# One hybrid decoder step on one core: convolution taps dealt differently, the conv norm's channel sums one block later, the key turns placed among the chunk sums, and the GLA gate multiplied in ahead of its norm

## The chip, the cores and the metric

The kernel runs on one core of a Trainium2 chip. The metric is device microseconds of one launch. Everything is in f32; the products of activations with weights split each operand into a high part (type fp32r) and a rest and use three products.

## The reference, cut to what matters

There are 1024 prompt tokens and 8 sample tokens (T = 1032 columns). One layer is computed:

```python
proj = rms_norm(x) @ w_in          # c_val, c_gate, q, k, v, r, a_lr
u = c_val * sigmoid(c_gate)
conv = silu(layer_norm(depthwise_conv31(u) + b_dw))
log_a = log_sigmoid(a_lr @ w_alpha + b_alpha) / 16
o, S = gla(q / 8, k, v, log_a)     # S_t = diag(a_t) S_(t-1) + k_t v_t^T, o_t = q_t S_t
o = rms_norm(o, gla_g) * silu(r)   # per head of 128
x = x + concat(conv, o) @ w_out
x = x + cross_attn(rms_norm(x), memory keys, memory values)
x = x + relu(rms_norm(x) @ w_up)**2 @ w_down
y = rms_norm(x)
```

The gate silu(r), the gain gla_g and the factor of the norm are multiplied element by element, so that their order changes rounding alone.

## The kernel before, in words

Activations stand with features on the 128 partitions and the 1032 tokens along the free axis, in three blocks of 344 columns. A weight tile is [128, 8, 128]: 8 steps k over the input features, for 128 output features. A tile product is 8 x 3 x 3 = 72 matmuls into three banks of PS[0] or PS[1]. Each engine's program is written out by hand, in order, with semaphores between them.

For each weight tile t, SyncE (SP) loads it, ScalarE (ACT) makes the high part (`w_high`, L620) and GpSimd (POOL) the rest in two halves (`lo`, L557) into one of two slots, t % 2. `w_high(t)` waits until the product of tile t-2 is done, since it takes over that slot. In the stage of the output projection (tiles T_OUT to T_OUT+7) `w_high(t+2)` is the last thing that `residual_tile(t)` does on ACT, behind VectorE's (DVE) addition of tile t to the residual (L1745), ACT's operand copy and ACT's square.

**Input projection.** 21 tiles (I_A at 8, I_K 9, I_Q 11, I_V 13, I_R 17), each three blocks of 24 matmuls (`in_block`, L1162). `SLOTS` names what TensorE (PE) does between the blocks. From tile I_V on, each tile's blocks 1 and 2 are followed by a "unit": eight matmuls of 128 x 128 (`unit_scores`, L1132, 16 records) that give the GLA scores of one level of a binary tree for one pair of heads, in two banks M[0] and M[1], one per half g. A unit's half needs the bank that the half of the unit before left: DVE frees it for units 0 to 11 with a masked copy (`level_select`, L1633), ACT for units 12 to 15 (`block_select`, L798). DVE's `unit_step` is an update of q (L1609 to L1612), a select, an update of k (L1620) and the second select.

**Convolution.** 124 taps on DVE (4 channel tiles of 31, `TAPS`), each one instruction over 128 x 1024 (L1559 to L1563). `taps(n)` does the next n. Their counts decide what DVE does before which unit: 24 in the last round of `u_product`, 4 before `decay_tree`, 16 ahead of unit 0, and then 1, 5, 1, 5, 1, 5, 1, 5, 1, 7 behind units 0 to 9. Behind unit 10 come the sums over the four channel tiles (L1675 to L1677), which PE sums over the partitions (`channel_sum`, L1121, "mean" in SLOTS at tile I_R+2, block 0); behind unit 11 DVE centres (L1681), ACT squares (L850), DVE adds (L1689), PE sums again ("var", tile I_R+3, block 0), ACT makes the factor (L853, L854), DVE multiplies it in (L1693, behind unit 14) and ACT does the silu (L858).

**Between the projections.** PE turns the keys (`key_turn`, L1148, four of four transposes), ACT reads them to k_in (L682), PE makes each chunk's k v product (`chunk_sum`, L1231, 8 chunks), DVE the recurrent states (`state_after`, L1704 and L1708), PE the outputs (`outputs`, L1249 and L1251, four rounds of two chunks). DVE and ACT read each round to sc_t (L1717, L874) and ACT squares it into sq_t (L880). ACT copies the conv result as operand (`conv_high`, L862), POOL makes its rest (L573) and then the sample tokens' state: two products (L581), two (L586) and two sums (L589).

**GLA norm and output projection.** PE does, in this order: k 0 to 3 of tile T_OUT (the conv half); the sample outputs (`sample_out`, L1283); 12 products with ones that give the sums of squares of the 4 heads (L1294, one per block of 344, alternating between M[0] and M[1]); k 0 to 3 of tile T_OUT+1; k 4 to 7 of T_OUT, then k 4 to 7 of T_OUT+1; the six further tiles. ACT takes 12 logarithms (L892) and 4 exponentials (L897). Then, per head, DVE multiplies o by the factor (L1731, L1732), by gain and gate (L1735), ACT copies the high part (L902) and DVE makes the rest (L1490), which PE's k = 4 + h waits for. SP loads the residual x once the last gate is done.

## Time and profile before

| | us |
|---|---|
| three runs | 1565.95, 1568.66, 1574.23 (median 1568.66) |
| profiled execution, its own time | 1565.79 |
| its span | 1564.0 |
| PE busy | 1475.6 (94%) |
| PE weight loads busy | 1430.9 (91%) |
| DVE, ACT, POOL busy | 610.2 (39%), 451.9 (29%), 383.2 (25%) |
| mean granted clock of PE | 0.979 of full speed |

PE is busy from end to end but for the first tenth and for a stretch between some 250 and 470 us. A matmul shows its latency there, so that "busy" is not the array at its peak: PE's pace is read from how far apart its groups start. In the views below, times run from the start of the span.

### The profile page before, as it was taken

What the parts mean: (1) busy time and instruction counts of PE and PEld (TensorE: products, weight loads), DVE (VectorE), ACT (ScalarE), POOL (GpSimd) and SP (SyncE); (2) the same over time, 40 slices, a digit from 0 to 9 for tenths busy, and PEclk for the clock granted to TensorE, in tenths of its full rate; (3) what the DMA queues carried; (4) which work ended last, traced back from release to release, by engine and by line L of the source; (5) the groups of instructions that cost most, each with busy time, mean ns of one, the idle gap of its engine ahead of it and who ended that gap; (6) DMA issues with size and microseconds to landing.
All of it is one profiled execution on the core that took longest, in us unless ns stands there. A gap on an engine that the chain in (4) does not pass through costs nothing.

```text
span 1564.0 us, 22310 instructions
## 1 busy us (share of the span) xinstructions
PE 1475.6 (94%) x9454; PEld 1430.9 (91%) x9454; DVE 610.2 (39%) x649; ACT 451.9 (29%) x598; POOL 383.2 (25%) x292
## 2 busy tenths in 40 slices
PE   5899998998989999788999999999999999999994
PEld 5799997997769999677999999999999999999994
DVE  3759989895243345462231211122011211022123
ACT  5532252438252233341233211123011311022121
POOL 5753231213302222100222222222222222222220
PEclk9999999999989999999999999999999999999997
DMA  8411150012033341336111111111111111111102
GB/s 293 141 61 48 58 51 28 28 41 68 31 122 122 109 155 55 121 128 230 55 41 42 52 54 40 41 54 40 54 41 51 42 54 40 54 40 40 54 27 108
DMA packets 45273, 113.99 MB, mean 73 GB/s; under 512 B 7688, under 2 KB 20248, under 8 KB 43808
## 3 DMA queue, kind: packets, MB, share of 16 engines
q1 hardware_dynamic: 43312, 104.19, 21.0%
q10 hardware_dynamic: 1904, 8.98, 1.4%
q8 instruction: 44, 0.72, 0.2%
q14 instruction: 13, 0.11, 0.0%
HBM read 100.85 MB, written 12.30 MB: 72 GB/s over the span
## 4 chain that ended last, share of the span: by engine, by line
PE 80%; DVE 7%; issue 5%; ACT 3%; POOL 3%; DMA 1%; ACTq 0%; SPq 0%; DVEq 0%; POOLq 0%
PE ps L1061 63%; PE ps L1162 10%; DVE ps L1561 2%; POOL w_split L557 2%; PE m L1132 1%; PE m L1325 1%; PE ps L1359 1%; PE ps L1175 1%; ACT w_split L620 1%; DMA cache_b<-in_cache_v 1%; DVE x_res L1934 1%; POOL a_op L573 0%; DMA v_raw<-out_mv 0%; PE ps L1381 0%; DVE x_in L1527 0%
## 5 line engine op out<-in xcount | busy, mean ns | idle before, releaser
L557 POOL TENSOR_TENSOR w_split<-w_raw,w_split 128x512 fp32r<-128x512 f32 x234 | 324.8, 1409 | 1122.3 <-ACT w_split L620 1122.2
L1061 PE MATMUL ps<-a_op,w_split 128*128 128x344 f32 x3456 | 548.8, 321 | 8.1 <-DVE a_op L1490 6.3
L1061 PEld LDWEIGHTS ps<-a_op,w_split 128*128 128x128 f32 x3456 | 545.9, 189 | 9.9 <-issue 5.5
L1061 PE MATMUL ps<-b_op,w_split 128*128 128x344 f32 x2880 | 454.6, 319 | 0.0
L1061 PEld LDWEIGHTS ps<-b_op,w_split 128*128 128x128 f32 x2880 | 452.3, 188 | 0.8 <-issue 0.4
L1162 PE MATMUL ps<-a_op,w_split 128*128 128x344 f32 x1440 | 233.8, 322 | 0.0
L1162 PEld LDWEIGHTS ps<-a_op,w_split 128*128 128x128 f32 x1440 | 227.1, 188 | 1.9 <-issue 1.4
L620 ACT ACTIVATE w_split<-w_raw 128x1024 fp32r<-128x1024 f32 x117 | 122.8, 1050 | 239.3 <-PE ps L1061 239.1
L1561 DVE SCALAR_TENSOR_TENSOR ps<-conv_in,par,ps 128x1024 f32<-128x1024 f32 x116 | 149.6, 1290 | 3.7
L1905 DVE SCALAR_TENSOR_TENSOR tmp<-ps,rstd 128x1032 f32<-128x1032 f32 x32 | 39.5, 1233 | 215.1 <-PE ps L1061 203.2
L1915 DVE TENSOR_TENSOR x_res<-x_res,ps 128x1032 f32 x24 | 29.5, 1230 | 230.8 <-PE ps L1061 230.8
L1015 ACT ACTIVATE tmp<-tmp 128x1032 f32<-128x1032 f32 x32 | 34.1, 1067 | 259.1 <-DVE tmp L1905 259.1
L1745 DVE TENSOR_TENSOR x_res<-x_res,ps 128x1032 f32<-128x1032 f32 x24 | 29.5, 1229 | 163.6 <-PE ps L1061 163.6
L1061 PE MATMUL ps<-m_op,w_split 128*128 128x256 f32 x384 | 55.5, 304 | 21.9 <-POOL w_split L557 21.9
L1061 PEld LDWEIGHTS ps<-m_op,w_split 128*128 128x128 f32 x384 | 51.7, 208 | 25.1 <-issue 18.1
L1910 DVE TENSOR_TENSOR a_op<-tmp,a_op 128x1032 f32 x32 | 39.5, 1234 | 80.7 <-ACT a_op L1018 80.7
L909 ACT ACTIVATE b_op<-x_res,par 128x1032 fp32r<-128x1032 f32 x16 | 18.6, 1160 | 128.4 <-DVE x_res L1745 128.4
L666 ACT ACTIVATE tmp<-x_res 128x1032 f32<-128x1032 f32 x21 | 22.2, 1057 | 66.0 <-DVE x_res L1745 66.0
L1018 ACT ACTIVATE a_op<-tmp 128x1032 f32 x32 | 34.2, 1067 | 4.3
L1325 PE MATMUL m<-k_op,a_op 128*128 128x256 f32 x192 | 26.2, 292 | 6.7 <-ACT ex L944 6.7
L1325 PEld LDWEIGHTS m<-k_op,a_op 128*128 128x128 f32 x192 | 25.0, 197 | 7.8 <-ACT ex L944 7.2
L557 POOL TENSOR_TENSOR w_split<-w_more,w_split 128x512 fp32r<-128x512 f32 x16 | 25.0, 1586 | 16.3 <-ACT w_split L620 16.3
(200 smaller groups left out, 924.2 us busy)
## 6 DMA issues: line engine op xcount, KB each, us to landing
w_raw<-in_wt SPq DMA_DIRECT2D x117, 512.0 KB, 3.5
...
```

The costliest lines, as they stand in the source:

```text
L557: gp.tensor_tensor(w_split[:, slot, 1, part, :], src, w_split[:, slot, 0, part, :].bitcast(F32), ALU.subtract).then_inc(w_low_done, 1)
L620: act.activation(w_split[:, slot, 0, :, :], src, ACT.Copy).then_inc(w_high_done, 1)
L1015: act.activation(tmp[:, j, :], tmp[:, j, :], ACT.Square).then_inc(scalar_step, 1)
L1018: act.activation(dst, tmp[:, j, :], ACT.Copy).then_inc(hidden_high, 1)
L1061: last = pe.matmul(ps[:, b, 0:w], w_split[:, slot, wp, k, :], src[:, k, xp, c0:c0 + w], start=(k == 0 and j == 0), stop=(k == KT - 1 and j ...
L1162: last = pe.matmul(PS[0][:, b, 0:CB], w_split[:, p % 2, wp, k, :], a_op[:, k, xp, b * CB:(b + 1) * CB], start=(k == 0 and j == 0), stop=(k ...
L1325: last = pe.matmul(bank[:, i * MEM:(i + 1) * MEM], a_op[:, 2 * h + k, qp, c0:c0 + C], k_op[:, h % 2, kp, k, :], start=(k == 0 and j == 0), ...
L1561: link(dve.scalar_tensor_tensor(out=conv_acc, in0=src, scalar=t_, in1=conv_acc, op0=ALU.mult, op1=ALU.add))
L1745: dve.tensor_tensor(cols(x_res[:, m, :]), cols(x_res[:, m, :]), pcols(t % 2), ALU.add).then_inc(ps_free, 1)
L1905: dve.scalar_tensor_tensor(out=cols(tmp[:, j, :]), in0=pcols((T_FF + j) % 2), scalar=0.0, in1=cols(rstd[:, :]), op0=ALU.max, op1=ALU.mult) ...
L1910: dve.tensor_tensor(dst, tmp[:, j, :], hi, ALU.subtract).then_inc(hidden_low, 1)
L1915: dve.tensor_tensor(x, x, pcols((T_FF + j) % 2), ALU.add).then_inc(ps_free, 1)
```

## The change

Four things change: where `taps` come (26, 4, 10 ahead of unit 0 where it was 24, 4, 16; then 1, 5, 1, 5, 1, 5, 1, 6, 1, 7, 3 behind units 0 to 10); "mean" and "var" one block later, and the conv norm's multiplication behind unit 15; the order of key turns and chunk sums on PE with ACT's reads and silus to match; and the GLA part, where o, gain and gate are multiplied into r_t first and the norm's factor last, with the 12 sums in the big banks (three banks to a logarithm) and the conv halves of both tiles behind them, and k 4 to 7 of the two tiles taken in turns.

```diff
--- before.py
+++ after.py
@@ -82,8 +82,8 @@
 MISC = {name: n for n, name in enumerate(
     [name for p in range(T_OUT) for b in range(NB) for name in SLOTS.get((p, b), ()) if name[0] != "v"]
     + [("kt", g) for g in range(4)] + [("smp", 0)])}
-SLOTS.setdefault((PLACE["in", I_R + 2], 0), []).append(("mean",))
-SLOTS.setdefault((PLACE["in", I_R + 3], 0), []).append(("var",))
+SLOTS.setdefault((PLACE["in", I_R + 2], 1), []).append(("mean",))
+SLOTS.setdefault((PLACE["in", I_R + 3], 1), []).append(("var",))
 
 
 UNITS = []
@@ -456,7 +457,8 @@
                     sp.dma_start(o["gla_p"], state[:, NC_ - 1, :, :]).then_inc(gla_states_stored, 16)
                     sp.wait_ge(sample_state, 2)
                     sp.dma_start(o["gla_s"], st_smp.rearrange("p a (s v) -> p a s v", s=NS)).then_inc(gla_states_stored, 16)
-                    sp.wait_ge(gla_gated, 3 * H)
+                    sp.wait_ge(gla_products, 2 * H)
+                    sp.wait_ge(gla_square, 2 * NR + H)
                     sp.dma_start(x_res[:, 0:2, :], a["x"][:, 0:2, :]).then_inc(x_res_loaded[0], 16)
                     sp.dma_start(x_res[:, 2:KT, :], a["x"][:, 2:KT, :]).then_inc(x_res_loaded[1], 16)
                 if T_OUT + 3 <= t < T_XQ + 3:
@@ -848,26 +850,34 @@
                             if m == 3:
                                 act.wait_ge(centered_summed, 2)
                             act.activation(ln_sum if m == 0 else ln_sq[m - 1], conv_y[:, m, :], ACT.Square).then_inc(centered_square, 1)
-                    if (i, b) == (I_R + 3, 0):
+                    if (i, b) == (I_R + 3, 1):
                         act.wait_ge(var_ready, 1)
                         link(act.activation(cols(ln_sum), pcols(1), ACT.Ln, bias=small[:, 128:129], scale=1.0 / DC))
                         act.activation(ln_sum, ln_sum, ACT.Exp, scale=-0.5).then_inc(ln_scale_ready, 1)
-                    if (i, b) == (I_R + 3, 1):
-                        for m in range(CT):
-                            act.wait_ge(conv_normed, m + 1)
-                            act.activation(conv_y[:, m, :], conv_y[:, m, :], ACT.Silu, bias=par[:, P_LNB + m:P_LNB + m + 1],
-                                           scale=par[:, P_LNG + m:P_LNG + m + 1]).then_inc(conv_silu, 1)
+
+            def key_read(g):
+                read(("kt", g), lambda b: b[:, :].rearrange("p (c a n) -> p c a n", c=2, a=2), k_in[:, 2 * g:2 * g + 2, :, :])
+
+            def silu(m):
+                act.wait_ge(conv_normed, m + 1)
+                act.activation(conv_y[:, m, :], conv_y[:, m, :], ACT.Silu, bias=par[:, P_LNB + m:P_LNB + m + 1],
+                               scale=par[:, P_LNG + m:P_LNG + m + 1]).then_inc(conv_silu, 1)
+
             def conv_high(m):
                 act.wait_ge(conv_silu, m + 1)
                 act.activation(a_op[:, m, 0, :], conv_y[:, m, :], ACT.Copy).then_inc(operand_high, 1)
 
+            key_read(0)
+            key_read(1)
+            silu(0)
+            key_read(2)
+            silu(1)
+            key_read(3)
+            silu(2)
+            silu(3)
             act.wait_ge(tile_done, T_OUT)
-            conv_high(0)
-            conv_high(1)
-            for g in range(4):
-                read(("kt", g), lambda b: b[:, :].rearrange("p (c a n) -> p c a n", c=2, a=2), k_in[:, 2 * g:2 * g + 2, :, :])
-            conv_high(2)
-            conv_high(3)
+            for m in range(CT):
+                conv_high(m)
 
             for r in range(NR):
                 act.wait_ge(gla_out, r + 1)
@@ -886,20 +896,15 @@
             for h in range(H):
                 if h == 2:
                     act.wait_ge(gla_states_stored, 32)
-                for j in range(NB):
-                    n_ = NB * h + j
-                    act.wait_ge(gla_sum, n_ + 1)
-                    act.activation(lnv[:, h, j * CB:(j + 1) * CB], M[n_ % 2][:, 0:CB], ACT.Ln, bias=small[:, 128:129],
-                                   scale=1.0 / DV).then_inc(gla_sum_read, 1)
-            act.wait_ge(gla_sum, NB * H)
+                act.wait_ge(gla_sum, h + 1)
+                act.activation(cols(lnv[:, h, :]), pcols((h + 1) % 2), ACT.Ln, bias=small[:, 128:129],
+                               scale=1.0 / DV).then_inc(gla_sum_read, 1)
             for h in range(H):
-                act.wait_ge(gla_sum_read, NB * (h + 1))
+                act.wait_ge(gla_sum_read, h + 1)
                 act.activation(sq_t[:, h, :], lnv[:, h, :], ACT.Exp, scale=-0.5).then_inc(gla_rstd, 1)
             for h in range(H):
-                act.wait_ge(gla_gated, 3 * (h + 1))
-                if h >= 2:
-                    act.wait_ge(gla_low, h - 1 if h == 2 else h)
-                act.activation(a_op[:, CT + h, 0, :], sq_t[:, h, :], ACT.Copy).then_inc(operand_high, 1)
+                act.wait_ge(gla_gated, h + 1)
+                act.activation(a_op[:, CT + h, 0, :], r_t[:, h, 0:T], ACT.Copy).then_inc(operand_high, 1)
             act.wait_ge(gla_states_stored, 32)
 
             def residual_tile(t, m, gain, n_op, n_sq):
@@ -1218,9 +1223,6 @@
                         in_block(i, b)
                     between(T_IN + i, b)
 
-            pe.wait_ge(k_updated, 14)
-            for g in range(4):
-                key_turn(g)
             def chunk_sum(c):
 
                 if c % 2 == 0:
@@ -1252,11 +1254,18 @@
                                              q_t[p0:p0 + DK, pair, NS + C * c:NS + C * (c + 1)], start=False, stop=True)
                 last.then_inc(gla_out, 1)
 
+            pe.wait_ge(k_updated, 14)
+            key_turn(0)
+            key_turn(1)
             pe.wait_ge(ps_free, T_OUT)
+            chunk_sum(0)
+            chunk_sum(1)
+            key_turn(2)
+            chunk_sum(2)
+            chunk_sum(3)
+            key_turn(3)
             for g in range(2):
                 wait_read(pe, ("unit", N_UNITS - 1, g))
-            for c in range(4):
-                chunk_sum(c)
             pe.wait_ge(q_updated, 16)
             pe.wait_ge(ln_scale_ready, 1)
             for r in range(NR):
@@ -1268,10 +1277,6 @@
             def wait_conv(k):
                 pe.wait_ge(conv_low, k + 1)
 
-
-            pe.wait_ge(gla_even_read, NR)
-            pe.wait_ge(gla_odd_read, NR)
-            tile_product(T_OUT, T_OUT % 2, a_op, ALL, wait_conv, range(0, CT))
 
             pe.wait_ge(sample_state, 2)
             pe.wait_ge(sample_kq_ready, 1)
@@ -1287,19 +1292,25 @@
 
             pe.wait_ge(gla_square, 2 * NR + H)
             pe.wait_ge(sample_out_read, 1)
-            for n_ in range(H * NB):
-                h, j = divmod(n_, NB)
-                if n_ >= 2:
-                    pe.wait_ge(gla_sum_read, n_ - 1)
-                pe.matmul(M[n_ % 2][:, 0:CB], ones[:, :], sq_t[:, h, j * CB:(j + 1) * CB], start=True, stop=True).then_inc(gla_sum, 1)
+            pe.wait_ge(gla_even_read, NR)
+            pe.wait_ge(gla_odd_read, NR)
+            for h in range(H):
+                if h >= 2:
+                    pe.wait_ge(gla_sum_read, h - 1)
+                for b in range(NB):
+                    last = pe.matmul(PS[(h + 1) % 2][:, b, 0:CB], ones[:, :], sq_t[:, h, b * CB:(b + 1) * CB], start=True, stop=True)
+                last.then_inc(gla_sum, 1)
 
 
             def wait_gla(k):
                 pe.wait_ge(gla_low, k - CT + 1)
 
-            tile_product(T_OUT + 1, (T_OUT + 1) % 2, a_op, ALL, no_wait, range(0, CT))
-            for t in (T_OUT, T_OUT + 1):
-                tile_product(t, t % 2, a_op, ALL, wait_gla, range(CT, KT))
+            for j, t in enumerate((T_OUT, T_OUT + 1)):
+                pe.wait_ge(gla_sum_read, 3 + j)
+                tile_product(t, t % 2, a_op, ALL, wait_conv, range(0, CT))
+            for k in range(CT, KT):
+                for t in (T_OUT, T_OUT + 1):
+                    tile_product(t, t % 2, a_op, ALL, wait_gla, range(k, k + 1))
             for m in range(2, KT):
                 t = T_OUT + m
                 tile_product(t, t % 2, a_op, ALL, no_wait)
@@ -1643,7 +1654,7 @@
             link(dve.memset(conv_in[:, :, 0:CW - 1], 0.0))
             for m in range(CT):
                 u_product(m)
-                taps(16 if m < 3 else 24)
+                taps(16 if m < 3 else 26)
             dve.wait_ge(softplus_ready, 1)
             dve.scalar_tensor_tensor(out=la[:, :, :], in0=la[:, :, :], scalar=0.0, in1=lnz,
                                      op0=ALU.min, op1=ALU.subtract).then_inc(log_a_ready, 1)
@@ -1653,7 +1664,7 @@
             dve.memset(qz[0], 0.0).then_inc(qz_zeroed, 1)
             dve.wait_ge(conv_states_stored, 32)
             dve.memset(qz[1][:, :], 0.0).then_inc(qz_zeroed, 1)
-            taps(16)
+            taps(10)
             wait_in_tile(dve, I_V - 1)
             link(dve.tensor_copy(small[:, 64:80].rearrange("p (a s) -> p a s", a=2), k_t[:, :, 0:NS]))
             link(dve.memset(small[:, 80:112], 0.0))
@@ -1666,10 +1677,7 @@
             dve.wait_ge(masks_ready, 1)
             for u in range(N_UNITS):
                 unit_step(u)
-                if u < 9:
-                    taps(5 if u % 2 else 1)
-                if u == 9:
-                    taps(7)
+                taps((1, 5, 1, 5, 1, 5, 1, 6, 1, 7, 3)[u] if u <= 10 else 0)
                 if u == 10:
                     assert n_taps == len(TAPS)
                     link(dve.tensor_tensor(ln_sum, conv_y[:, 0, :], conv_y[:, 1, :], ALU.add))
@@ -1687,10 +1695,9 @@
                     else:
                         dve.wait_ge(centered_summed, m)
                         dve.tensor_tensor(ln_sum, ln_sum, ln_sq[m - 1], ALU.add).then_inc(centered_summed, 1)
-                if u == 14:
-                    dve.wait_ge(ln_scale_ready, 1)
-                    for m in range(CT):
-                        dve.tensor_tensor(conv_y[:, m, :], conv_y[:, m, :], ln_sum, ALU.mult).then_inc(conv_normed, 1)
+            dve.wait_ge(ln_scale_ready, 1)
+            for m in range(CT):
+                dve.tensor_tensor(conv_y[:, m, :], conv_y[:, m, :], ln_sum, ALU.mult).then_inc(conv_normed, 1)
 
             def state_after(c):
                 dve.wait_ge(chunk_kv, c + 1)
@@ -1719,25 +1726,42 @@
                 for c in (2 * r + 4, 2 * r + 5):
                     if c < NC_:
                         state_after(c)
+            def gate_prompt(h):
+                wait_in_tile(dve, I_R + h)
+                dve.wait_ge(gla_even_read, NR)
+                dve.wait_ge(gla_odd_read, NR)
+                r3 = r_t[:, h, NS:T].rearrange("p (c n) -> p c n", n=C)
+                dve.scalar_tensor_tensor(out=r3, in0=sc_t[:, h // 2, :, h % 2, :], scalar=par[:, P_GLAG:P_GLAG + 1],
+                                         in1=r3, op0=ALU.mult, op1=ALU.mult).then_inc(gla_products, 1)
+
+            gate_prompt(0)
+            gate_prompt(1)
             bank, b, _ = misc(("smp", 0))
             wait_full(dve, ("smp", 0))
             dve.tensor_copy(small[:, 160:192], bank[:, 0:32]).then_inc(sample_out_read, 1)
-
-            for h in range(H + 1):
-                if h < H:
-                    dve.wait_ge(gla_rstd, h + 1)
-                    dve.wait_ge(sample_out_read, 1)
-                    s3 = sq_t[:, h, NS:T].rearrange("p (c n) -> p c n", n=C)
-                    dve.tensor_tensor(s3, s3, sc_t[:, h // 2, :, h % 2, :], ALU.mult).then_inc(gla_gated, 1)
-                    dve.tensor_tensor(sq_t[:, h, 0:NS], sq_t[:, h, 0:NS], o_cols(h), ALU.mult).then_inc(gla_gated, 1)
-                    wait_in_tile(dve, I_R + h)
-                    dve.wait_ge(gla_gated, 3 * h + 2)
-                    dve.scalar_tensor_tensor(out=sq_t[:, h, :], in0=sq_t[:, h, :], scalar=par[:, P_GLAG:P_GLAG + 1],
-                                             in1=r_t[:, h, 0:T], op0=ALU.mult, op1=ALU.mult).then_inc(gla_gated, 1)
-                if h >= 1:
-                    if h == 3:
-                        dve.wait_ge(gla_low, 2)
-                    low(a_op[:, CT + h - 1, 1, :], sq_t[:, h - 1, :], None, a_op[:, CT + h - 1, 0, :], operand_high, 20 + h).then_inc(gla_low, 1)
+            gate_prompt(2)
+            gate_prompt(3)
+            dve.wait_ge(sample_out_read, 1)
+            for h in range(H):
+                dve.scalar_tensor_tensor(out=r_t[:, h, 0:NS], in0=o_cols(h), scalar=par[:, P_GLAG:P_GLAG + 1],
+                                         in1=r_t[:, h, 0:NS], op0=ALU.mult, op1=ALU.mult).then_inc(gla_products, 1)
+
+            def gate(h):
+                dve.wait_ge(gla_rstd, h + 1)
+                dve.wait_ge(gla_products, 2 * H)
+                dve.tensor_tensor(r_t[:, h, 0:T], r_t[:, h, 0:T], sq_t[:, h, :], ALU.mult).then_inc(gla_gated, 1)
+
+            def gla_rest(h):
+                low(a_op[:, CT + h, 1, :], r_t[:, h, 0:T], None, a_op[:, CT + h, 0, :], operand_high, 21 + h).then_inc(gla_low, 1)
+
+            gate(0)
+            gate(1)
+            gla_rest(0)
+            gate(2)
+            gla_rest(1)
+            gate(3)
+            gla_rest(2)
+            gla_rest(3)
 
             def residual_tile(t, m, gain, n_op, n_sq):
 
```

## Rows read from the trace of the kernel before

**Rows 1.** Timeline of PE, 244 to 377 us: start, length, work, [idle before, releaser].

```profile
258.21 3.75 PE L1132 MATMUL m<-qz,k_t 128*128 128x128 f32 x16 [7.60 <-DVE sc_t L1633]
261.62 4.46 PE L1162 MATMUL ps<-a_op,w_split 128*128 128x344 f32 x24
...
345.59 1.97 PE L1121 MATMUL ps<-rstd,ones 128*128 128x344 f32 x6 [0.75 <-DVE rstd L1677]
...
363.60 2.00 PE L1121 MATMUL ps<-rstd,ones 128*128 128x344 f32 x6 [1.10 <-DVE rstd L1689]
...
374.81 1.95 PE L1132 MATMUL m<-qz,k_t 128*128 128x128 f32 x16
```

**Rows 2.** Timeline of DVE, 219 to 376 us.

```profile
219.68 2.31 DVE L1648 SCALAR_TENSOR_TENSOR la<-la,tmp 128x2064 f32<-128x2064 f32 x1 [3.10 <-ACT tmp L829]
...
234.76 21.09 DVE L1561 SCALAR_TENSOR_TENSOR ps<-conv_in,par,ps 128x1024 f32<-128x1024 f32 x16
...
325.06 0.72 DVE L1633 COPY_PREDICATED sc_t<-mask,m 128x512 f32<-128x512 int8 x1 [1.56 <-PE m L1132]
...
339.73 1.23 DVE L1675 TENSOR_TENSOR rstd<-conv_y 128x1032 f32<-128x1032 f32 x1
341.00 2.20 DVE L1676 TENSOR_TENSOR rstd<-rstd,conv_y 128x1032 f32<-128x1032 f32 x1
...
371.83 4.66 DVE L1693 TENSOR_TENSOR conv_y<-conv_y,rstd 128x1032 f32<-128x1032 f32 x4
```

**Rows 3.** Timeline of PE, 377 to 468 us.

```profile
379.68 1.06 PE L1148 MATMUL m<-ident,k_t 128*128 128x128 f32 x8 [2.92 <-ACT sc_t L798]
...
389.77 1.28 PE L1249 MATMUL ps<-sc_t,v_tok 128*128 128x128 f32 x10
...
393.90 1.99 PE L1231 MATMUL ps<-v_tok,k_in 128*128 128x256 f32 x8
...
418.20 5.93 PE L1061 MATMUL ps<-a_op,w_split 128*128 128x344 f32 x36 [0.79 <-DVE sc_t L1717]
423.98 4.59 PE L1283 MATMUL m<-small,st_smp 128*128 128x2 f32 x32
429.38 10.42 PE L1294 MATMUL m<-sq_t,ones 128*128 128x344 f32 x24 [0.82 <-ACT sq_t L884]
...
449.46 2.21 PE L1061 MATMUL ps<-a_op,w_split 128*128 128x344 f32 x9 [4.01 <-DVE a_op L1490]
...
456.93 10.38 PE L1061 MATMUL ps<-a_op,w_split 128*128 128x344 f32 x54 [0.84 <-DVE a_op L1490]
467.66 2.59 PE L1061 MATMUL ps<-a_op,w_split 128*128 128x344 f32 x15 [0.35 <-POOL w_split L557]
```

**Rows 4.** Timeline of DVE: the states of chunks 0 to 3, first addition to the residual.

```profile
385.90 1.25 DVE L1704 COPY state<-ps 64x128 f32<-64x128 f32 x4 [8.21 <-PE ps L1231]
387.27 4.66 DVE L1708 SCALAR_TENSOR_TENSOR state<-state,small,ps 64x128 f32<-64x128 f32 x12
...
461.77 1.23 DVE L1745 TENSOR_TENSOR x_res<-x_res,ps 128x1032 f32<-128x1032 f32 x1 [2.46 <-PE ps L1061]
```

**Rows 5.** Timeline of ACT, 378 to 446 us.

```profile
378.96 1.06 ACT L798 ACTIVATE sc_t<-m 64x512 f32<-64x512 f32 x2
...
441.69 3.94 ACT L897 ACTIVATE sq_t<-lnv 128x1032 f32<-128x1032 f32 x4
```

**Rows 6.** Timeline of POOL, 340 to 403 us.

```profile
340.71 3.64 POOL L557 TENSOR_TENSOR w_split<-w_raw,w_split 128x512 fp32r<-128x512 f32 x2 [12.04 <-ACT w_split L620]
...
400.64 2.36 POOL L589 TENSOR_TENSOR st_smp<-st_smp,vb 128x1024 f32<-128x1024 f32 x1
```

**Rows 7.** Windows: busy us of engines (instructions), PEclk granted, DMA share, GB/s.

```profile
390.00:418.00 28.00, 27.42 (x136) 20.17 (x134) 9.89 (x25) 5.78 (x10) 13.01 (x7) 1.00 0.11 43
430.00:432.00 2.00, 2.00 (x5) 1.12 (x4) 0.00 (x0) 1.18 (x2) 0.00 (x0) 0.50 0.00 0
450.00:454.00 4.00, 2.52 (x11) 2.07 (x10) 3.87 (x5) 1.06 (x1) 0.00 (x0) 0.54 0.00 0
```

1 line of the change is left out of this document (added).

## The prediction

> **What bounds the kernel now.** I read PE's timeline first, because PE is busy in 94% of the span: only its gaps and its slow stretches can give time. They lie between 250 and 468 us. PE waits 7.60 us for DVE's first masked copy (L1633) ahead of unit 1, and that unit then takes 3.75 us where a unit takes 1.95 (as the last one at 374.81) [rows 1]. It waits 0.75 us for the first channel sums and 1.10 for the second [rows 1]. From the end of unit 15 (374.81 + 1.95 = 376.76) [rows 1] to the first output at 389.77 it needs 13.0 us, and from the end of the outputs (418.20 - 0.79 = 417.4) to the start of tile T_OUT+2 at 467.66 it needs 50.3 us [rows 3]. The other engines' timelines [rows 2, 4, 5, 6] say what PE waits for, and the windows [rows 7] at what clock it runs: 1.00 during the outputs, 0.50 in the middle of the GLA sums, 0.54 after the wait of 4.01 us at 449.46. Ahead of 250 us nothing is changed; behind 467.66 the same tiles run back to back, so that each us won before is a us of the end.
>
> **A. Taps.** DVE does 16 taps from 234.76 in 21.09 us [rows 2], 1.318 each. Six fewer there is 7.9 us. The two extra ones in the last round of u_product cost 2.6 us and end inside the 3.10 us that DVE waits for ACT's softplus ahead of 219.68 [rows 2]: nothing (at most 2.6 if ACT's chain moved, which nothing here does). Unit 0's second masked copy then ends at about 251.9. PE's block ends at 258.21 - 7.60 = 250.6; unit 1 takes 1.8, waits about 0.5 in its middle and ends at 252.9 in place of 258.21 + 3.75 = 261.96: 9.0 us. The next block took 4.46 us from first to last; the clock was at its low level there, and I book 0.3. **A gives 9.3 us** (bounds: 7.6, the wait alone, and 9.8).
> Is DVE late elsewhere? It starts 7.9 us earlier, PE 9.3 us. The 1.4 us are taken up by its short waits for PE in the next units. The extra tap behind unit 7 (1.3 us) is hidden by the 1.56 us that DVE waits ahead of unit 9's first copy at 325.06 [rows 2].
>
> **B. Three more taps behind unit 10, sums one block later.** The taps take 3.95 us, and the channel sums follow them. PE reaches "mean" a block (24 records at the 5.93 / 36 = 0.165 us of [rows 3], 3.9 us) and a unit (1.95) later, so that it need not wait for the sums any more; 0.75 and 1.10 us go. What is late next is unit 11's masked copies, which stand on DVE behind the sums: PE wants them for unit 12, which it now reaches without the mean's 1.97 and the 0.75 us before it. How long the three sums take decides. L1675 takes 1.23 us, L1676 with the same shape 2.20, and it began while POOL was in `lo` (340.71, 3.64 us) [rows 2, 6]. In the new order POOL's `lo` runs while DVE is at the three taps, which read PSUM and do not slow down beside POOL (the 16 of [rows 2] did not); so I take 1.23 each. By that PE waits 0.7 us at unit 12; if they stay at 2.20 it waits 2.6. **B gives 1.85 - 0.7 = 1.15 us** (bounds: -0.8 and 1.85). "Var" has about 2 us to spare one block later: nothing.
>
> **C. From unit 15 to the outputs.** PE waits for ACT's block_select (its first half 0.5 of 1.06 us [rows 5]) as now, but no longer for the silus between: 1.4 us in place of 2.92. Then two turns 1.06 us [rows 3], two chunk sums 1.99 [rows 3], and a turn 0.5. Now the norm's multiplication (4.66 us [rows 2]) stands on DVE between unit 15 and the first state; before, DVE waited 8.21 us there [rows 4]. It starts as unit 15 is in, and the first of the four meets POOL's `lo`, for which I add 1.2 as at L1676: it ends 7.2 us after unit 15. With the first state's 1.25 us [rows 4], chunk sum 2 may start at 8.5, chunk sum 3 (behind a state of 4.66 / 3 = 1.55 [rows 4]) at 10.2; with it and the last turn the outputs start at 11.7. The waits are as dense as those of before, so that I add 0.5 for the clock: 12.2 us against 13.0. **C gives 0.8 us** (bounds: -1.0, with low clock for all the 6.1 us of work, and 2.3 with no meeting and no clock loss).
> ACT's key_read(3) now waits for the last turn, so its silus 2 and 3 and four operand copies end some 6.8 us after the outputs' start. POOL follows: four rests and the sample chain, whose last sum now ends at 400.64 + 2.36 = 403.0 [rows 6], come to about 2 us before sample_out wants them. DVE and ACT read the first output round late, but PE needs those banks only in the third round. Nothing, with 2 us to spare.
>
> **D. From the outputs to tile T_OUT+2.** In the times of before: sample_out follows at once, 417.4 + 4.6 = 422.0. The first two products o x gain x gate (1.3 us each) are on DVE in its shadow. ACT's squares take 0.9 as now. The 12 products with ones took 10.42 us as 24 records [rows 3]; at the channel sums' pace (1.97 for 6) they are 7.9. Their clock was low at 430 to 432 [rows 7] behind the small sample matmuls, which they still follow: I take 4 us of low clock, 1.7 us lost, and no more waits for logarithms, since one of 1032 columns takes about 1 us, as an exponential does [rows 5], against 2.0 for three products. End 432.5. Two conv halves of 5.93 [rows 3]: 444.4. Under them go the last logarithm, four exponentials of 0.99 [rows 5], two gates, the first copy and rest: the first rest is ready 8.8 us after the sums, 3 before PE wants it, and each further one every 2.5 us against 2.96 for a pair of k steps. So the waits of 4.01 and 0.84 us, one between them and the low clock among them go [rows 3, 7]. The GLA halves are 72 records at 0.165: 11.9 us. T_OUT ends at 454.8, T_OUT+1 at 456.3.
> **What is late next is the weight slot.** T_OUT+2 needs it from T_OUT. Before, T_OUT was done at about 461.6, DVE's addition began at 461.77 [rows 4], ACT's copy, square and w_high and POOL's `lo` followed, and PE went on at 467.66, released by POOL [rows 3]: 6.05 us, of which 5.9 were covered by T_OUT+1's GLA half. Taken in turns, T_OUT+1 covers only 1.5 us. So PE stands 4.5 us, until 460.8, and after such a gap its clock was low ([rows 3, 7], 4.01 us and then 0.54), which I price at 1.7 us. **D gives 467.7 - 462.5 = 5.1 us** (bounds: 2.5, with a longer chain on ACT, and 7.5 without either loss of clock).
> SP's load of x moves ahead of all this; its 4 MB used to run beside the handover and no longer do: nothing either way. The extra wait of SP holds back only T_OUT+3's weights, wanted 12 us later.
>
> **Sum.** 9.3 + 1.15 + 0.8 + 5.1 = 16.3 us. The profiled execution took 1565.79 us (span 1564.0 and 1.8 around it), which gives 1549.5. The median of the three runs is 2.9 us above the profiled one, the lowest 0.2 above; I take the middle: **1551 us**.
>
> **Where page and trace may part.** In the trace the clock fell in the stretch of key turns, but it held many gaps, and the outputs ran at 1.00 [rows 7]. The Trainium skill, "TensorE: Matmul & The Clock Gate", Part 4, says of a transpose that it does not count as PE activity in the same way. By that rule turns strewn among the chunk sums would keep the clock low for the whole of C, which is C's lower bound and the first half of the last rival; no row separates turns from gaps.
>
> **Rivals.**
> 1. The handover gives all back: PE's stall is 6 us, with low clock behind it for longer, and D gives 1 to 2 us. For it: 4.5 us are lost by my own count. Gain 12.5: 1555. Chance 0.13.
> 2. POOL's sample chain is late: each of its four rests takes 0.7 us more (DVE's norm runs beside it) and the chain starts late; at 5 us over the spare 2, sample_out waits 3. Against: the rests ran beside DVE's states before too. Gain 13: 1554.5. Chance 0.09.
> 3. Clock low through C, but not beyond, with B at its lower bound: gain 12.5, 1555. Chance 0.09.
> 4. The change does not do what it says in A: DVE's 7.9 us are taken again, because unit 0's or 1's masked copy meets something else (ACT's copy of q, POOL), and PE still waits 4 us there. Gain 8 to 10: 1558.5. Chance 0.07.
> 5. Slower. If the clock is at its low level when the outputs start and their small matmuls (28 us, 128 columns, half of them over 64 rows) do not lift it, they take up to twice as long: +27.6 us against the 16.3, 1579. It decides from 60% of the outputs at the low clock. For it: C's work comes in bits. Against: PE came out of the same stretch to 1.00 for 390 to 418 [rows 7]. Chance 0.04.
> The forecast itself has 0.58.
>
> **Range and chances.** The four terms' bounds do not fall together; gains of 11 to 21 against the runs shown make 1545 to 1558, which takes in rivals 1 to 3. Half a per cent, 7.8 us, is about what a measurement here can tell from no change: faster means below 1560.8. Forecast, rivals 1 to 3 and most of 4 are there: 0.90; 0.05 within; 0.05 slower.
>
> **What would show it.** PE's wait ahead of unit 1 below 1 us; a wait under 1 us at unit 12 and L1676 at 1.23; outputs starting near 378 and ending near 406; no wait between the sums (9 to 10 us in all) and none ahead of any GLA k step; then one wait of 4 to 5 us released by POOL's w_split, with a low clock behind it; the chain behind it unchanged. The prediction is wrong if that wait is absent or twice as long, if PE stands ahead of sample_out or if the outputs take over 30 us.

## The result and the profile after

| | before | after |
|---|---|---|
| median of four runs, us | 1569.82 (1565.95 to 1574.23) | 1550.20 (1548.92 to 1552.48) |
| profiled execution, its own time | 1565.79 | 1552.48 |
| its span | 1564.0 | 1550.8 |

The ratio is 0.9874, with an interval of 0.9848 to 0.9899: faster by 1.3%, 19.6 us between the medians and 13.3 between the two profiled executions. The forecast was 1551.

The timeline of PE in the kernel after. The columns are start, duration of the group, engine, line, operation, tiles, shapes, count, and in brackets the idle time before it and what ended it. These lines answer to [rows 1, 3].

```profile
247.82 1.95 PE L1137 MATMUL m<-acc,k_t 128*128 128x128 f32 x16
253.39 1.05 PE L1137 MATMUL m<-qz,k_t 128*128 128x128 f32 x8
254.86 1.16 PE L1137 MATMUL m<-qz,k_t 128*128 128x128 f32 x8 [0.42 <-DVE sc_t L1644]
...
342.57 2.27 PE L1137 MATMUL m<-acc,k_t 128*128 128x128 f32 x16 [0.23 <-ACT qz L788]
344.68 1.90 PE L1126 MATMUL ps<-rstd,ones 128*128 128x344 f32 x6
...
366.86 1.95 PE L1137 MATMUL m<-qz,k_t 128*128 128x128 f32 x16
370.28 1.06 PE L1153 MATMUL m<-ident,k_t 128*128 128x128 f32 x8 [1.47 <-ACT sc_t L800]
371.68 3.29 PE L1233 MATMUL ps<-v_tok,k_in 128*128 128x256 f32 x8 [0.34 <-ACT k_in L684]
374.77 1.00 PE L1153 MATMUL m<-ident,k_t 128*128 128x128 f32 x4
377.57 1.10 PE L1233 MATMUL ps<-v_tok,k_in 128*128 128x256 f32 x4 [1.81 <-DVE state L1711]
379.08 2.07 PE L1233 MATMUL ps<-v_tok,k_in 128*128 128x256 f32 x4 [0.40 <-DVE state L1715]
380.94 1.06 PE L1153 MATMUL m<-ident,k_t 128*128 128x128 f32 x4
381.80 1.57 PE L1251 MATMUL ps<-sc_t,v_tok 128*128 128x128 f32 x10
...
409.67 3.87 PE L1288 MATMUL m<-small,st_smp 128*128 128x2 f32 x32
414.36 9.96 PE L1301 MATMUL ps<-sq_t,ones 128*128 128x344 f32 x24 [0.82 <-ACT sq_t L894]
423.89 23.07 PE L1066 MATMUL ps<-a_op,w_split 128*128 128x344 f32 x144
451.53 23.70 PE L1066 MATMUL ps<-a_op,w_split 128*128 128x344 f32 x132 [4.57 <-POOL w_split L559]
```

The wait of 7.60 us ahead of unit 1 is 0.42, in the unit's middle. Unit 12 waits 0.23 ahead of its first half and some 0.3 ahead of its second (2.27 us where a unit takes 1.95), and the channel sums (344.68) follow it without a wait. From 423.89 on, the two conv halves and the two GLA halves (144 records) run as one block, without the waits of 4.01 and 0.84 us and the one between them. Behind them stands the one new wait: 4.57 us, ended by POOL's rest of the weights for tile T_OUT+2.

The other engines at the same places (timelines of DVE, POOL and ACT in the kernel after), which answer to [rows 2, 4, 6]:

```profile
338.69 1.24 DVE L1684 TENSOR_TENSOR rstd<-rstd,conv_y 128x1032 f32<-128x1032 f32 x1
...
341.71 0.72 DVE L1644 COPY_PREDICATED sc_t<-mask,m 128x512 f32<-128x512 int8 x1
...
342.93 0.70 DVE L1644 COPY_PREDICATED sc_t<-mask,m 128x512 f32<-128x512 int8 x1
...
369.45 6.81 DVE L1700 TENSOR_TENSOR conv_y<-conv_y,rstd 128x1032 f32<-128x1032 f32 x4
445.66 1.23 DVE L1769 TENSOR_TENSOR x_res<-x_res,ps 128x1032 f32<-128x1032 f32 x1 [6.92 <-PE ps L1066]
369.73 4.29 POOL L559 TENSOR_TENSOR w_split<-w_raw,w_split 128x512 fp32r<-128x512 f32 x2 [12.51 <-ACT w_split L622]
405.02 2.35 POOL L591 TENSOR_TENSOR st_smp<-st_smp,vb 128x1024 f32<-128x1024 f32 x1
449.00 1.04 ACT L622 ACTIVATE w_split<-w_raw 128x1024 fp32r<-128x1024 f32 x1
```

The second channel sum on DVE takes 1.24 us in place of the 2.20 of [rows 2]. The two masked copies of unit 11 end at 342.43 and 343.63, and each frees the bank for a half of unit 12. The profile puts unit 12's wait down to ACT's `qz` (L788), but that is the copy for unit 13, of the other pair; unit 12 reads `acc`, which was copied some 7 us earlier, so that the wait is for DVE's masked copy. The norm's multiplication, now beside POOL's `lo`, takes 6.81 in place of 4.66. POOL's sample chain ends at 407.37, 2.3 us before PE takes up the sample outputs at 409.67. And the handover of the weight slot can be followed: addition at 445.66, ACT's high part done at 450.04, POOL's first half behind it, PE on at 451.53.

The clock in windows of the kernel after (the columns: window and its length, busy time of PE, PEld, DVE, ACT and POOL with counts, then the granted clock, the DMA share, GB/s). They answer to [rows 7].

```profile
372.00:375.00 3.00, 3.00 (x10) 2.29 (x9) 3.00 (x2) 1.16 (x2) 2.03 (x1) 0.53 1.20 223
378.00:381.00 3.00, 2.60 (x9) 1.70 (x8) 2.34 (x7) 0.00 (x0) 0.00 (x0) 0.66 0.00 0
384.00:409.00 25.00, 25.00 (x121) 18.30 (x121) 7.62 (x19) 9.85 (x14) 21.43 (x10) 1.00 0.14 56
415.00:419.00 4.00, 4.00 (x8) 2.36 (x7) 1.78 (x6) 1.40 (x2) 0.00 (x0) 0.50 0.30 66
452.00:456.00 4.00, 4.00 (x16) 4.00 (x16) 2.86 (x2) 1.71 (x2) 2.84 (x3) 0.50 0.54 205
```

The clock is low in parts of the stretch of turns and chunk sums, in the first half of the GLA sums, and behind the new wait. The outputs run at 1.00 from 384 on.

Since PE is the bound, the time can be laid out by landmarks on its timeline. All later tables use these stages, in us, each from one profiled execution: **start** up to unit 0; **A** from there to the first value turn; **B** on to the end of unit 15; **C** to the first output; **outs** the outputs; **D** on to the start of tile T_OUT+2; **E** on into the sums of the stage behind the output projection (their third product); **rest**.

| | start | A | B | C | outs | D | E | rest | span |
|---|---|---|---|---|---|---|---|---|---|
| before | 244.9 | 21.0 | 110.9 | 13.0 | 27.7 | 50.2 | 80.6 | 1015.7 | 1564.0 |
| after | 247.8 | 11.8 | 109.2 | 13.0 | 27.9 | 41.8 | 83.3 | 1015.9 | 1550.8 |
| gain | -2.9 | 9.2 | 1.7 | 0.0 | -0.3 | 8.4 | -2.7 | -0.2 | 13.2 |

Without the start, which the change does not touch, the gain is 16.1 us; the sum forecast was 16.3. The 2.9 us of the start are taken up under the experiments.

### The profile page after: what moved, and what is told of

It reads as the page before. It is cut to its first block, busy times and chain, and to the rows that moved or that the text cites. A ratio compares the mean times of both kernels' runs of the same rounds, so it can differ in the third digit from the quotient of the medians.

```text
span 1550.8 us, 22307 instructions
## 1 busy us (share of the span) xinstructions
PE 1475.2 (95%) x9454; PEld 1432.9 (92%) x9454; DVE 610.9 (39%) x649; ACT 450.4 (29%) x590; POOL 386.3 (25%) x292
## 4 chain that ended last, share of the span: by engine, by line
PE 82%; DVE 7%; issue 4%; ACT 3%; POOL 2%; DMA 2%; ACTq 0%; SPq 0%; DVEq 0%; POOLq 0%
PE ps L1066 64%; PE ps L1167 11%; DVE ps L1572 2%; PE m L1137 1%; POOL w_split L559 1%; PE m L1336 1%; PE ps L1370 1%; PE ps L1180 1%; DMA cache_b<-in_cache_v 1%; DVE x_res L1958 1%; ACT w_split L622 0%; POOL a_op L575 0%; DMA v_raw<-out_mv 0%; PE ps L1392 0%; DVE x_in L1538 0%
## 5 line engine op out<-in xcount | busy, mean ns | idle before, releaser
L1066 PEld LDWEIGHTS ps<-m_op,w_split 128*128 128x128 f32 x384 | 54.2, 217 | 25.1 <-issue 18.1
L1934 DVE TENSOR_TENSOR a_op<-tmp,a_op 128x1032 f32 x32 | 39.5, 1234 | 80.7 <-ACT a_op L1023 80.7
L1502 DVE SCALAR_TENSOR_TENSOR b_op<-x_res,par,b_op 128x1032 fp32r<-128x1032 f32 x16 | 21.3, 1330 | 19.7 <-ACT b_op L914 19.7
## 6 DMA issues: line engine op xcount, KB each, us to landing
cache_b<-in_cache_k SPq DMA_DIRECT2D x2, 2048.0 KB, 10.5
```

What stands on the lines that cost most here:

```text
L1066: last = pe.matmul(ps[:, b, 0:w], w_split[:, slot, wp, k, :], src[:, k, xp, c0:c0 + w], start=(k == 0 and j == 0), stop=(k == KT - 1 and j ...
L1934: dve.tensor_tensor(dst, tmp[:, j, :], hi, ALU.subtract).then_inc(hidden_low, 1)
```

## The experiments

My theory: the four parts add up, each through its own stage, and the one new cost is the handover of the slot (D) with the low clock behind it (E). The rivals: a part is carried by another part; the order of the turns matters by itself; the move of the sums by a block is worth nothing, or far more. Each kernel below is the changed one with one part undone, or carried further. They ran in three groups, each on one chip, with "before" beside them: the changed kernel again, halves in sequence, taps and GLA part (median of before 1568.1 us); turns first, sums in block 0, norm dealt and the first run of both (1571.6); both again and the copy moved (1569.8). I compare ratios between groups, medians within one, and stages for the place.

**The changed kernel again.**

> The changed kernel once more, as the reference of this group. Theory (four separate terms): 1550 us, within 3. What is open is the stage before 245 us, which the change leaves alone and where unit 0 began 2.9 us later in the changed kernel's profile than in the kernel before (247.82 against 244.89). Theory: that is the loading of the first weights, which differs from execution to execution, so that here unit 0 begins anywhere between 244.5 and 248.5. Rival: the change caused it; then it begins at 247.5 to 248.2 again.

Measured: 1551.13 us, ratio 0.9884 (0.9848 to 0.992), stages as after to 0.1 us but for the start, 248.5.

**Halves in sequence.** Only the order of k 4 to 7 is undone.

```diff
-            for k in range(CT, KT):
-                for t in (T_OUT, T_OUT + 1):
-                    tile_product(t, t % 2, a_op, ALL, wait_gla, range(k, k + 1))
+            for t in (T_OUT, T_OUT + 1):
+                tile_product(t, t % 2, a_op, ALL, wait_gla, range(CT, KT))
```

> k 4 to 7 of tile T_OUT whole and then those of T_OUT+1, as in the kernel before; all else of the change stays. Theory (the weight slot of T_OUT+2 follows from T_OUT, 5.9 us after its end, and taking the two tiles in turns leaves only 1.5 us of it covered): PE's wait of 4.57 us ahead of T_OUT+2 goes to under 0.5, so does the low clock behind it (2.7 us), T_OUT+2 starts 37.5 to 38.5 us after the outputs' end in place of 41.9, and the time is 6 to 7 us less than the changed kernel's: 1543.5. The rests of heads 0 to 3 come 2.7, 2.0, 1.2 and 1.4 us before their k step wants them. Rival (taking turns is what hides the gates): PE waits 0.5 to 1.5 us at each of k 5, 6 and 7 and half the gain or more is lost, 1547 to 1550.

Measured: 1542.73 us, ratio 0.9843 (0.9806 to 0.9879). PE's timeline of this kernel:

```profile
405.37 5.85 PE L1288 MATMUL m<-small,st_smp 128*128 128x2 f32 x32
412.03 9.60 PE L1301 MATMUL ps<-sq_t,ones 128*128 128x344 f32 x24 [0.82 <-ACT sq_t L894]
421.21 23.04 PE L1066 MATMUL ps<-a_op,w_split 128*128 128x344 f32 x144
444.59 35.58 PE L1066 MATMUL ps<-a_op,w_split 128*128 128x344 f32 x225 [0.35 <-POOL w_split L559]
```

The 144 records take the same 23 us in either order: the operands of all four k steps are there in time. The wait behind them is 0.35 in place of 4.57, and E is back at 80.6. So taking the tiles in turns bought nothing and cost 4.2 us of stall and 2.7 us of low clock. That is 6.9 us by the stages; the medians of the group differ by 8.4. D is 39.2, above what was expected, since the sample outputs took 5.85 us here and 3.87 in the kernel after, on code that is the same in both.

**Taps as before.**

```diff
-                taps(16 if m < 3 else 26)
+                taps(16 if m < 3 else 24)
...
-            taps(10)
+            taps(16)
...
-                taps((1, 5, 1, 5, 1, 5, 1, 6, 1, 7, 3)[u] if u <= 10 else 0)
+                taps((1, 5, 1, 5, 1, 5, 1, 5, 1, 7, 0)[u] if u <= 10 else 0)
```

> The changed kernel with the tap counts of before (24, 4, 16 and 1, 5, 1, 5, 1, 5, 1, 5, 1, 7). Theory (term A stands by itself): PE waits about 7.6 us ahead of unit 1 and again runs at 1.2 GHz behind it, 9.3 us in all; the short wait at unit 12 (0.55 us) goes, since three taps fewer stand there; 8.5 to 9 us more than the changed kernel: 1559. Rival (the time is given back further down, because DVE is the engine that ends the stage): 1550 to 1553.

Measured: 1561.09 us, ratio 0.9952 (0.9939 to 0.9966). The line of unit 1 in this kernel:

```profile
259.08 3.33 PE L1137 MATMUL m<-qz,k_t 128*128 128x128 f32 x14 [7.59 <-DVE sc_t L1644]
```

The wait of [rows 1] is back whole; A is 21.4 (9.6 more than after) and B 0.7 less. The median is 10.0 us above that of the changed kernel in the same group; the stages A and B account for 8.9. B at 108.5 also gives the price of the three late taps: with the sums in block 1 they cost 0.7 us, and without them the later block (with the norm's multiplication behind unit 15) is worth 2.4 of B.

**GLA part as before.** The gate, gain and norm in their old order, 12 sums in M, one conv half ahead of sample_out, SP's load behind the last gate. Its core:

```diff
-                last.then_inc(gla_sum, 1)
+            for n_ in range(H * NB):
...
+                pe.matmul(M[n_ % 2][:, 0:CB], ones[:, :], sq_t[:, h, j * CB:(j + 1) * CB], start=True, stop=True).then_inc(gla_sum, 1)
...
-            for k in range(CT, KT):
-                for t in (T_OUT, T_OUT + 1):
-                    tile_product(t, t % 2, a_op, ALL, wait_gla, range(k, k + 1))
+            tile_product(T_OUT + 1, (T_OUT + 1) % 2, a_op, ALL, no_wait, range(0, CT))
+            for t in (T_OUT, T_OUT + 1):
+                tile_product(t, t % 2, a_op, ALL, wait_gla, range(CT, KT))
```

> The changed kernel with the GLA norm, gates and output halves in the order of before (terms A, B and C stay). Theory: from the outputs' end to T_OUT+2 it takes 50.3 us in place of 41.9, but the low clock behind T_OUT+2's wait (2.7 us) goes, so that D was worth 5.7 us and this takes 1556. Rival (the low clock is not the stall's doing, so that it stays): 1558.5. Second rival (the POOL sample chain is late and sample_out waits): more than 1559 with a wait ahead of L1283 or its like.

Measured: 1559.16 us, ratio 0.9939 (0.9921 to 0.9957). PE's timeline of this kernel has the waits of [rows 3] again, and one that stood between them:

```profile
438.60 2.09 PE L1070 MATMUL ps<-a_op,w_split 128*128 128x344 f32 x9 [4.00 <-DVE a_op L1503]
442.29 2.95 PE L1070 MATMUL ps<-a_op,w_split 128*128 128x344 f32 x9 [1.60 <-DVE a_op L1503]
446.07 10.44 PE L1070 MATMUL ps<-a_op,w_split 128*128 128x344 f32 x54 [0.83 <-DVE a_op L1503]
```

D is 50.2 and E 80.6, both as before, and no wait stands ahead of the sample outputs, so that neither rival came. The median is 3 us above the 1556 expected; the profiled execution, at 1555.35 the fastest of its ten, agrees with the expectation, and what the others lost was not seen. Against the changed kernel of the same group (1551.13) undoing the taps costs 10.0 us and undoing the GLA part 8.0, together 18.0, where the full change is worth 17.0 there. Within the noise of some us the two parts act in different places and add up. Of the GLA part, only the order of k 4 to 7 was undone by itself: what the gate ahead of the norm, the sums in the big banks and the moved conv half are worth each, no run separates.

**Key turns first, as before.** Four turns, then four chunk sums on PE; four reads, then four silus on ACT; the norm stays behind unit 15.

```diff
-            key_turn(0)
-            key_turn(1)
+            for g in range(4):
+                key_turn(g)
             pe.wait_ge(ps_free, T_OUT)
-            chunk_sum(0)
-            chunk_sum(1)
-            key_turn(2)
-            chunk_sum(2)
-            chunk_sum(3)
-            key_turn(3)
```

> The changed kernel with four key turns first and the chunk sums behind them on PE, and ACT's four key reads ahead of the four silus. Theory (stretch C is set by DVE, which does the norm's multiplication in 6.81 us and then the first state before chunk sum 2 may start; where the turns stand is worth nothing): from unit 15 to the outputs 11.3 to 12.5 us, as in the changed kernel (11.7 to 13.0), and 1550 us. POOL's sample chain ends some 5 us earlier against the outputs, since ACT need not wait for the last turn. Rival (turns among the sums take 1 us and more off the path): 1.0 to 2.0 us longer from unit 15 to the outputs, 1552.

Measured: 1551.57 us, ratio 0.9881 (0.9865 to 0.9897): the same as the changed kernel. C is 12.2. The line of the third and fourth chunk sums shows why:

```profile
376.77 3.63 PE L1229 MATMUL ps<-v_tok,k_in 128*128 128x256 f32 x8 [3.12 <-DVE state L1703]
```

Without turns in between PE waits 3.12 us for DVE's first state in place of 1.81. DVE's norm stands ahead of that state and sets the end of C in either order, so that the order of the turns is worth nothing that these runs can tell while it stands there.

**Channel sums in block 0, as before.** The taps stay as in the change.

```diff
-SLOTS.setdefault((PLACE["in", I_R + 2], 1), []).append(("mean",))
-SLOTS.setdefault((PLACE["in", I_R + 3], 1), []).append(("var",))
+SLOTS.setdefault((PLACE["in", I_R + 2], 0), []).append(("mean",))
+SLOTS.setdefault((PLACE["in", I_R + 3], 0), []).append(("var",))
```

> The changed kernel with mean and var back behind block 0, all else of the change kept, three taps behind unit 10 among it. Theory (term B is the price of the three late taps that the later block hides): PE waits 2.7 us ahead of the mean's sums and about 1.1 ahead of var's, and the stretch from the first value turn to the end of unit 15 takes 112.0 to 112.8 us in place of 109.2; 1553.5. Rival (the block makes no difference, since unit 11's copies bind either way): 109 to 110 us and 1550.5.

Measured: 1557.27 us, ratio 0.9916 (0.99 to 0.9931), some 5 us slower than the changed kernel by the ratios. PE's timeline:

```profile
340.96 3.43 PE L1126 MATMUL ps<-rstd,ones 128*128 128x344 f32 x6 [2.78 <-DVE rstd L1685]
343.68 4.72 PE L1167 MATMUL ps<-a_op,w_split 128*128 128x344 f32 x24
...
360.63 2.00 PE L1126 MATMUL ps<-rstd,ones 128*128 128x344 f32 x6 [1.10 <-DVE rstd L1697]
```

With the three late taps and the sums in block 0 PE waits 2.78 us at the mean, where it waited 0.75 before, and 1.10 at the variance, as before. The first of these waits brings the low clock: the six sums take 3.43 us in place of 1.90 and the block behind them 4.72 in place of 4.21. B is 114.6, 5.4 more than after. I had expected 2.8 to 3.6 more because I had priced the waits without the clock. The move by a block is what makes the taps behind unit 10 cheap: 0.7 us, by the kernel with the taps as before.

**Norm dealt among the states.** Not an undoing: the kernel with the turns first says that DVE's norm holds up C, so two of its four multiplications go behind the states.

```diff
-            for m in range(CT):
+            def conv_scale(m):
                 dve.tensor_tensor(conv_y[:, m, :], conv_y[:, m, :], ln_sum, ALU.mult).then_inc(conv_normed, 1)
 
+            conv_scale(0)
+            conv_scale(1)
...
                 state_after(c)
+                if c >= 2:
+                    conv_scale(c)
```

> The changed kernel, where DVE multiplies the norm's factor into channel tiles 0 and 1 only ahead of the states, into tile 2 behind the state of chunk 2 and into tile 3 behind that of chunk 3. Theory (DVE's norm is what PE waits for in C): PE's 1.81 us ahead of chunk sum 2 go to under 0.5, the stretch from unit 15 to the outputs takes 8.5 to 9.5 us in place of 11.7 to 13.0, and the time is 1547. Rival 1 (the clock, not DVE, makes that stretch long): over 11 us. Rival 2 (POOL's chain is then late): the stretch shortens, but a wait of 1 to 3 us stands ahead of sample_out and the time stays at 1549 to 1550.

Measured: 1549.25 us, ratio 0.9861 (0.9843 to 0.9879); 1547 was expected. It is 2.3 us below the kernel with the turns first, of the same group, with intervals that overlap. PE's timeline and two clock windows of this kernel:

```profile
372.19 1.10 PE L1233 MATMUL ps<-v_tok,k_in 128*128 128x256 f32 x4
373.69 1.13 PE L1233 MATMUL ps<-v_tok,k_in 128*128 128x256 f32 x4 [0.41 <-DVE state L1719]
...
403.05 6.99 PE L1288 MATMUL m<-small,st_smp 128*128 128x2 f32 x32 [0.31 <-POOL st_smp L591]
410.86 10.04 PE L1301 MATMUL ps<-sq_t,ones 128*128 128x344 f32 x24 [0.82 <-ACT sq_t L894]
```
```profile
404.00:408.00 4.00, 4.00 (x21) 4.00 (x20) 2.16 (x2) 0.72 (x2) 0.00 (x0) 0.50 0.56 231
408.00:412.00 4.00, 3.18 (x12) 2.79 (x13) 1.92 (x3) 1.68 (x5) 0.00 (x0) 0.50 0.00 0
```

The wait for the first state is gone and C is 8.3 in place of 13.0. But D grows by 3.6, to 45.4. The wait for POOL's sample chain explains 0.31 of it; the rest is the clock, which is at 0.50 through the whole of the sample outputs (6.99 us in place of 3.87). Three quarters of what C gains, D gives back. Read in windows of 1 us, the clock is low from 403.0 to 416.6 here, 13.7 us in one piece. In the kernel after it is low for 13.7 us as well, but in three pieces, 372.2 to 375.6 and 379.0 to 382.4 among the turns and sums, where PE waits in part, and 413.1 to 419.9. Between these two executions the low clock was not made longer; it moved to where PE is dense. That is no rule: other executions of the same stretch have it low for less, as the last section shows.

**Both**, the dealt norm and the halves in sequence, run in two groups:

> Both edits at once: the norm dealt among the states, and k 4 to 7 of T_OUT whole ahead of those of T_OUT+1. Theory (the two terms add up): 1542.7 less 3.2 is 1539.5. Rival (the POOL chain turns the first gain into a wait ahead of sample_out): 1542 to 1543.

> The same kernel as e6_dealt_norm_and_sequence, beside the one above on the same chip: 1540.5 by the run before, and how much the stretches from unit 15 to the outputs (8.31 us then) and from the outputs' end to the third output tile (39.5 us then) differ between executions of one kernel, which in the kernels so far moved with the granted clock of sample_out (3.87 to 6.99 us).

Measured: 1540.46 us, ratio 0.9809 (0.979 to 0.9828), and 1539.98, ratio 0.9819 (0.9798 to 0.984). C is 8.3, D 39.5 and E 80.6 in both executions. Against the halves in sequence alone that is 3.0 us by the stages (3.2 expected), but the low clock between unit 15 and the conv halves was also shorter here, 10.2 us in place of 13.7, so that not all of it is the dealt norm.

**The slot's high part behind the select**, on top of both:

```diff
                     if (i, b) == (N_IN - 1, LAST_BLOCK):
+                        w_high(T_IN + i + 2, i % 2)
```

(and `i < N_IN - 1` is added where `w_high` stood, ahead of the read of unit 15).

> This is e6_dealt_norm_and_sequence with one step moved: ACT's high-part copy of the second tile of the output projection stands behind its read of unit 15 (block_select) instead of ahead of it. Theory: in the changed kernel the first key turn waited 1.47 us for ACT's select, which stood behind that copy, and GpSimd's rest of the same tile met DVE's conv norm. With the copy behind, the first turn waits at most 0.6 us, the stretch from unit 15 to the first output goes from 8.3 to 7.0 to 7.6 us, and the time is 0.7 to 1.3 us below e6 of the same call (about 1539.5). Rival: the stretch is set by DVE (two multiplications of the norm and the first states), and a shorter wait ahead of the turns becomes a longer one ahead of the third chunk sum or of the outputs; no difference to e6. Second rival: the later copy holds up the key reads on ACT by 1 us and the second turns wait for them; 0.5 us slower than e6.

Measured: 1538.63 us, ratio 0.9802 (0.9788 to 0.9815), the fastest here, though its interval overlaps that of the kernel with both in the same group. PE's and DVE's timelines of this kernel:

```profile
368.93 1.09 PE L1155 MATMUL m<-ident,k_t 128*128 128x128 f32 x8 [0.79 <-DVE k_t L1632]
...
374.61 1.13 PE L1235 MATMUL ps<-v_tok,k_in 128*128 128x256 f32 x4 [0.40 <-DVE state L1720]
...
368.79 2.37 DVE L1702 TENSOR_TENSOR conv_y<-conv_y,rstd 128x1032 f32<-128x1032 f32 x2
371.71 1.25 DVE L1716 COPY state<-ps 64x128 f32<-64x128 f32 x4 [0.55 <-PE ps L1235]
```

The wait ahead of the turns, 1.47 us for ACT's select until then, is 0.79 (at most 0.6 expected) and now for DVE's last update of k, which ends 0.7 us sooner than the select did. The two multiplications of the norm are under way before POOL's halves begin (370.02) and take 2.37 us, in place of 3.45 in the kernel with both. DVE's first state then waits 0.55 us for PE's chunk sums, which it did not before. C goes from 8.3 to 7.9, where 7.0 to 7.6 was expected. So the theory is half right: the select was late, but a third of the 0.7 us won there goes to the next wait, 0.55 us for ACT's read of the keys in place of 0.34. The medians differ by 1.4 us, more than the 0.4 that the stages show.

| stages | start | A | B | C | outs | D | E | rest | span |
|---|---|---|---|---|---|---|---|---|---|
| halves in sequence | 245.2 | 11.8 | 109.2 | 11.7 | 27.6 | 39.2 | 80.6 | 1015.9 | 1541.1 |
| taps as before | 245.8 | 21.4 | 108.5 | 12.4 | 27.6 | 41.8 | 82.8 | 1016.4 | 1556.6 |
| GLA part as before | 245.5 | 11.8 | 109.2 | 12.4 | 27.7 | 50.2 | 80.6 | 1016.1 | 1553.6 |
| turns first | 247.0 | 11.8 | 109.2 | 12.2 | 27.7 | 41.8 | 83.2 | 1015.8 | 1548.7 |
| sums in block 0 | 247.5 | 11.8 | 114.6 | 12.4 | 27.7 | 41.8 | 83.0 | 1016.0 | 1554.6 |
| norm dealt | 245.8 | 11.8 | 109.2 | 8.3 | 27.6 | 45.4 | 83.3 | 1016.4 | 1547.9 |
| both | 246.0 | 11.8 | 109.2 | 8.3 | 27.7 | 39.5 | 80.6 | 1015.6 | 1538.7 |
| both, copy behind select | 247.2 | 11.8 | 109.2 | 7.9 | 27.7 | 39.5 | 80.6 | 1019.0 | 1542.8 |

The **start** has the same code in all of them and in "before", apart from two taps that end in DVE's wait, and takes 244.9 to 248.5 us from one execution to the next. So its 2.9 us in the two profiles compared first are no cost of the change. The 1019.0 us in the last row are one execution that took 1544.5 us where the other four of that kernel took 1538.4 to 1539.1. The clock accounts for most of it: between 671 and 721 us the granted clock is 0.86 there, and 0.97 in the same stretch of the kernel with both, and the 576 matmuls from 699.97 on take 93.42 us in place of 90.70.

## Why the prediction was right

The number was right, 1551 for 1550.2, and so were the mechanisms. That the sum comes so close (16.3 for 16.1 by the stages) is in part luck: B and D gave 0.5 and 0.6 us more than forecast, C gave 0.8 less. The sizes stand as follows.

**A (9.3 forecast, 9.2 measured).** DVE's six taps were the bound there. Unit 1 waits 0.42 us in its middle (0.5 forecast), and the block behind unit 1 takes 4.02 us, as a block at full clock does, in place of 4.46. The rival that DVE's time is taken again elsewhere (4) did not come. The kernel with the taps put back shows that the whole of A hangs on them.

**B (1.15 forecast, 1.7 measured).** The 0.75 and 1.10 us went. Unit 12 waits for unit 11's masked copies, as worked out, 0.23 us and then some 0.3 in its middle, in place of the 0.7 that I booked. Most of the remaining 0.4 us is in small shifts: each wait that went had also made the block ahead of it 0.14 us longer (4.01 against a pitch of 3.87), and the two groups of sums stand 0.1 us closer to what follows them. L1684 takes 1.24 us, so the claim that DVE's sums no longer meet POOL's `lo` held. What the forecast had no price for is the parts taken alone: with the late taps but the sums in block 0, B is 5.4 us longer; without the late taps it is 0.7 shorter.

**C (0.8 forecast, 0.0 measured in this execution).** Up to the fourth chunk sum it went as worked out: counted from the end of unit 15 (366.86 + 1.95 = 368.81) the norm ends at 7.45 us (7.2 forecast), the third sum starts at 8.8 (8.5) and the fourth at 10.3 (10.2). The term that was mis-sized is the clock: I added 0.5 us, but the fourth sum and the last turn ran at the low level (2.07 and 1.06 us, against 1.13 and 0.60 in the kernel with the halves in sequence), which put the outputs 1.3 us later. Where the code of that stretch is the same, C came out as 13.0, 13.0 and 11.7, and as 12.4 in each of the three kernels with the taps, the GLA part or the channel sums as before. The 12.2 forecast lies among these: the clock there is worth a range of 1.3 us and not one value, and that one execution or another falls on 12.2 says nothing for my 0.5. The norm itself took 6.81 us where I had 5.9: both of its multiplications that overlap POOL's two halves were slowed, not one.

On the page cited in the prediction (the Trainium skill, "TensorE: Matmul & The Clock Gate", Part 4): by that rule the clock would be low through the whole of C. It was low for 3.4 us of C in the kernel with the halves in sequence and for some 6 in the kernel after. With the norm dealt the turns stand among the chunk sums in the same order, and the clock is at 1.00 through all of C:

```profile
366.80:375.10 8.30, 5.97 (x33) 4.72 (x33) 7.78 (x15) 5.73 (x8) 4.30 (x2) 1.00 0.64 126
```

So turns strewn among sums did not by themselves bring the low clock here. In that kernel the longer wait among them is gone as well, which fits the gaps as the cause but does not prove it.

POOL's sample chain had 2.3 us to spare, 2 forecast (rival 2 did not come), and the outputs took 27.9 us, 0.3 more than before at the most: their first ten records took 1.57 us at the low level in place of 1.28 (rival 5 did not come). Rival 3 came in part: the clock was low in two pieces of C and took its gain, but not through the whole of it, and B was above what I had and not at its lower bound.

**D (5.1 forecast, 5.7 measured: 8.4 in D less 2.7 in E).** The stall for the weight slot is 4.57 us where I had 4.5, ended by the POOL instruction that I named. The low clock behind it cost 2.7 in place of 1.7, and the work ahead of it 1.6 us less than I had: the sample outputs 3.87 us in place of 4.6, ACT's squares and the sums together 10.4 in place of 10.5, and the 144 records 0.160 us each in place of 0.165 (0.7 in all). Rival 1, a stall of 6 us with D worth 1 to 2, did not come. The halves in sequence settle the cause: with the wait gone E is 80.6 us again.

**The offset.** The profiled executions differ by 13.3 us, 3.0 less than the sum, and the medians by 19.6. The start's 2.9 us make up the first difference; what the medians have beyond the sum is in no trace that was kept. I had put the forecast between the profiled execution and the median of before, and this spread of some 3 us is what that choice was worth.
